# An encoder layer with product-key experts: two token tiles' heads chosen inside the query slabs, and the products' scratch laid out by tile

## The reference, cut to what matters

```python
q = jnp.einsum('td,de->te', x, wq).reshape(T, PEER_HEADS, 2, PEER_DHALF)       # 8 heads, 2 halves of 128
s = jnp.einsum('thcd,hcnd->thcn', q, keys).astype(jnp.float32)                 # 128 keys a half
v1, i1 = lax.top_k(s[:, :, 0], PEER_TOPK)                                      # 16 of each half
v2, i2 = lax.top_k(s[:, :, 1], PEER_TOPK)
cand = (v1[..., :, None] + v2[..., None, :])                                   # 256 sums
top_s, pos = lax.top_k(cand, PEER_TOPK)                                        # 16 of them
idx = i1 * N_KEYS + i2                    # of the 16 chosen; 8 x 16 = 128 experts a token
a = jnp.einsum('td,tkd->tk', xt, u_tab[it])                                    # u_tab: 16384 x 2048
hid = gelu(a) * softmax(top_s)
peer = jnp.einsum('tk,tkd->td', hid, v_tab[it])
x2 = layer_norm(alpha * x1 + peer)
```

## Time and profile before

| | |
|---|---|
| median of three runs | 3742.63 us (3737.31 to 3744.31) |
| the profiled execution | 3735.37 us |
| its span | 3733.6 us, mean granted TensorE clock 0.82 of full speed |
| busy share of the span | PE 66%, PE's weight loads 51%, DVE 74%, ACT 9%, POOL 33% |
| DMA | 1332.43 MB, mean 357 GB/s |

### The profile page before, as it was taken

One profiled execution on the slowest core, in us unless ns is written; L12 is line 12 of the kernel. 1 busy time (PEld: TensorE's weight loads), 2 busy tenths in 40 slices (PEclk: granted clock), 3 DMA queues, 4 the chain that ended last, 5 costly groups with the idle time before them and its releaser, 6 DMA issues.

```text
span 3733.6 us, 30440 instructions
## 1 busy us (share of the span) xinstructions
PE 2471.0 (66%) x11208; PEld 1892.2 (51%) x11208; DVE 2762.9 (74%) x3210; ACT 332.7 (9%) x832; POOL 1246.5 (33%) x1273
## 2 busy tenths in 40 slices
PE   7798799978975777959988999999978000000000
PEld 7687689545743444535677877777767000000000
DVE  5331220979989997787789889976655999988888
ACT  1212311000002221000100000000000000000000
POOL 2420000122233332223222223232222577777772
PEclk9899899988986657989999999999999555555555
DMA  8774355898998999989999999999998999999998
GB/s 245 219 232 121 143 190 179 292 397 332 341 405 343 406 419 375 422 343 414 421 422 423 423 423 423 423 421 424 423 382 336 413 407 410 409 390 370 392 373 348
DMA packets 297908, 1332.43 MB, mean 357 GB/s; under 512 B 70752, under 2 KB 136832, under 8 KB 146336
## 3 DMA queue, kind: packets, MB, share of 16 engines
q0 software_dynamic: 138624, 945.22, 62.9%
q1 hardware_dynamic: 126400, 371.83, 26.7%
q10 hardware_dynamic: 32736, 13.44, 1.4%
HBM read 1282.60 MB, written 57.20 MB: 359 GB/s over the span
## 4 chain that ended last, share of the span: by engine, by line
PE 35%; DMA 27%; DVE 22%; POOL 8%; issue 6%; another core or an unknown queue 1%; ACT 1%; ACTq 1%; SPq 0%; DVEq 0%; POOLq 0%
PE low L1559 18%; DMA arena<-in_ut 16%; PE low L1900 10%; DVE arena L1375 7%; DVE acc L1391 5%; DMA arena<-in_peer_v,arena 5%; POOL arena L611 4%; POOL arena L620 4%; DMA arena<-in_w 2%; DMA arena<-in_peer_u,arena 2%; PE low L1633 1%; PE acc L1633 1%; DMA arena<-y_scratch_b 1%; DVE low L1391 1%
## 5 line engine op out<-in xcount | busy, mean ns | idle before, releaser
L1391 DVE SCALAR_TENSOR_TENSOR acc<-arena,acc 128x2048 f32<-128x2048 f32 x443 | 1042.6, 2354 | 262.4 <-DMA arena<-in_peer_v,arena 226.7
L1559 PE MATMUL low<-arena 128*128 128x192 f32 (+1 forms) x4096 | 1064.8, 420 | 100.6 <-DMA arena<-in_w 77.3
L1900 PE MATMUL low<-arena 128*128 128x256 f32 x4096 | 915.5, 383 | 110.1 <-DMA arena<-in_ut 109.0
L1559 PEld LDWEIGHTS low<-arena 128*128 128x128 f32 x4096 | 738.3, 196 | 376.0 <-DMA arena<-in_w 74.6
L1900 PEld LDWEIGHTS low<-arena 128*128 128x128 f32 x4096 | 774.1, 191 | 251.3 <-DMA arena<-in_ut 133.2
L611 POOL DMA_INDIRECT arena<-in_peer_v,arena x576 | 579.5, 1006 | 924.3 <-DVE acc L1391 772.6
L1375 DVE SCALAR_TENSOR_TENSOR arena<-arena,acc 128x2048 f32<-128x2048 f32 x320 | 724.8, 2284 | 115.3 <-DMA arena<-in_peer_u,arena 107.6
L611 POOL DMA_INDIRECT arena<-in_peer_u,arena x320 | 320.1, 1000 | 1185.6 <-DVE arena L1375 856.1
L1391 DVE SCALAR_TENSOR_TENSOR low<-arena,low 128x2048 f32<-128x2048 f32 x126 | 296.6, 2354 | 35.8 <-DMA arena<-in_peer_v,arena 26.8
L620 POOL DMA_INDIRECT arena<-expert_scratch,arena x256 | 263.3, 1029 | 83.2 <-issue 83.2
L872 ACT COPY arena<-low 128x256 f32<-128x256 f32 x128 | 47.6, 372 | 971.0 <-PE low L1900 957.9
(11 more groups left out here) (274 smaller groups left out, 1678.3 us busy)
## 6 DMA issues: line engine op xcount, KB each, us to landing
arena<-in_w SPq DMA_DIRECT2D x128, 1024.0 KB
arena<-in_ut SPq DMA_DIRECT2D x128, 1024.0 KB
expert_scratch<-arena SPq DMA_DIRECT2D x128, 128.0 KB
arena<-in_peer_v,arena POOLq DMA_INDIRECT x576
arena<-toeplitz_scratch SPq DMA_DIRECT2D x64, 128.0 KB, 3.6
arena<-c_scratch SPq DMA_DIRECT2D x64, 128.0 KB, 4.2
bias_scratch<-distance_scratch SPq DMA_DIRECT2D x1, 5120.0 KB, 23.4
x_scratch<-arena ACTq DMA_DIRECT2D x5, 1024.0 KB
```

Of the source, the lines that this page charges most:

```text
L1391: stt(held, slot[j], wv_, held, ALU.mult, ALU.add).then_inc(used, 1)
L1559: ins = mm(L[n % 2][:, 0:width], wring[n % 2][:, k, :], rhs(k), start=k == 0, stop=k == KT - 1)
L1900: ins = mm(L[j % 4][:, 0:NSD], ud[j % 4][:, k, :], lane(catB, k)[:, P:NB], start=k == 0, stop=k == KT - 1)
```

## The change

1. **Tile 0.** A quarter of the scores is computed as soon as its four query slabs are out: `quarter(t, c)` stands inside slabs 4, 8 and 12 of the 16 (counted from 0), behind their fifth matmul, and after the last. The quarters go to PSUM banks `L[2]` and `L[3]` in turn instead of `acc`. DVE waits for a quarter, chooses its two heads and decodes them, and works no row before all eight are done; then 56 rows follow ahead of the scan, where 14 stood between the heads and 28 behind. Slots 2 and 3 may hold rows from row 2 on instead of row 16.
2. **Tile 2.** The same in group B's query slabs. DVE works 11 rows and, ahead of each pair of heads, 9; the heads are decoded one by one (`decode_head`) instead of in one `decode` with rows between its steps. POOL waits for each head of tile 2 as for those of tile 0 (`chosen`).
3. **The products' scratch** has tile 3's products in its first 8 MB and tile 4's in the second, each [expert in block][block][token]. ACT copies two blocks into one of two buffers, and SP stores the pair at once: 64 DMAs of 256 KB in pieces of 1 KB. The index of a product is computed to match (`idxe`, `tok_off`).
4. **The five loads of `early_sums`** stand at blocks 92, 98, 104, 110 and 116 instead of all at 116.
5. **ACT's root** of the second norm of tile 0 stands behind the 122nd block of the products instead of the 126th.

The diff, cut:

```diff
@@ -97,7 +97,7 @@
 NR = len(ROWS)
-SLOT_FROM = [0, 0, TOPK, TOPK, STEPS[0] + 6, R_U2 + 16]
+SLOT_FROM = [0, 0, 2, 2, STEPS[0] + 6, R_U2 + 16]
@@ -132,6 +132,11 @@
     return u % 3 if u < NUA else u % 2
+def chosen(t, h=PH - 1):
+    return {0: h + 1, 1: PH + 1, 2: PH + 2 + h, 3: 2 * PH + 2, 4: 2 * PH + 3}[t]
@@ -286,7 +291,7 @@
         ud = [at(WO + D * j, D).rearrange("p (k e) -> p k e", k=KT) for j in range(4)]
-        astg = [at(H2 + D + NSD * j, NSD) for j in range(4)]
+        astg = [at(H2 + D + 2 * NSD * j, 2 * NSD).rearrange("p (u n) -> p u n", u=2) for j in range(2)]
@@ -304,7 +309,7 @@
         vscr = nc.dram_tensor("v_scratch", [2, P, D], F32).ap()
-        ascr = nc.dram_tensor("expert_scratch", [EB * P * NSD, 1], F32).ap()
+        ascr = nc.dram_tensor("expert_scratch", [2 * P * EB * P, 1], F32).ap()
@@ -524,31 +530,39 @@
                 sp.dma_start(ud[j % 4].rearrange("p k e -> p (k e)"), a["ut"][j]).then_inc(ud_in[j % 4], 16)
-            def products_out(j):
-                sp.wait_ge(a_out, j + 1)
-                sp.dma_start(ascr.rearrange("(j p t) o -> j p (t o)", p=P, t=NSD)[j], astg[j % 4]
-                             ).then_inc(a_st[j % 4], 16)
+            def products_out(b):
+                sp.wait_ge(a_out, 2 * b + 2)
+                sp.dma_start(ascr.rearrange("(u p b n) o -> b p u (n o)", u=2, p=P, n=2 * P)[b], astg[b % 2]
+                             ).then_inc(a_st[b % 2], 16)
             def early_sums():
-                sp.wait_ge(idx_ready, PH + NT - 1)
+                sp.wait_ge(idx_ready, chosen(NT - 1))
                 sp.wait_ge(v_stored, 32)
                 sp.dma_start(x1f[0], x1scr[0]).then_inc(early_in, 16)
+                yield
                 sp.dma_start(vsum[0], vscr[0]).then_inc(early_in, 16)
+                yield
                 sp.dma_start(x1f[1][0:TS], x1scr[1, 0:TS, :]).then_inc(early_in, 16)
+                yield
                 sp.dma_start(vsum[1][0:TS], vscr[1, 0:TS, :]).then_inc(early_in, 16)
+                yield
                 sp.dma_start(vsum[2][0:TS], vscr[1, TS:P, :]).then_inc(early_in, 16)
+                yield
+            sums = early_sums()
             for j in range(EB):
                 experts_in(j)
-                if j >= 4:
-                    products_out(j - 4)
-                if j == EB - 12:
-                    early_sums()
+                if j >= 5 and j % 2:
+                    products_out((j - 5) // 2)
+                if j in range(EB - 36, EB - 11, 6):
+                    next(sums)
...
-            for j in range(EB - 4, EB):
-                products_out(j)
+            for b in range(EB // 2 - 2, EB // 2):
+                products_out(b)
@@ -593,9 +607,12 @@
                     if s % TOPK == 0:
-                        pool.wait_ge(idx_ready, s // TOPK + 1)
+                        pool.wait_ge(idx_ready, chosen(0, s // TOPK))
+                elif kind == "u" and t == 2:
+                    if s % TOPK == 0:
+                        pool.wait_ge(idx_ready, chosen(2, s // TOPK))
                 elif s == 0 and kind == "u" or i == R_V3 or i == R_V4:
-                    pool.wait_ge(idx_ready, PH + t)
+                    pool.wait_ge(idx_ready, chosen(t))
@@ -837,10 +854,18 @@
                 act.dma_start(x1scr[t], x1s[t]).then_inc(x1_stored, 16)
+            def quarter(t, c):
+                act.wait_ge(score_done, 4 * t + c + 1)
+                if t == NGA and not c:
+                    act.wait_ge(x1_stored, 16 * NT)
+                ins = nc.scalar.copy(scored[t][:, 512 * c:512 * c + 512], L[2 + c % 2])
+                ins.then_inc(quarter_out, 1)
+                if c == 3:
+                    act.wait_ge(quarter_out, 4 * (t // 2) + 4)
+                    act.sem_inc(score_out, 1)
             def scores(t):
                 src = acc if t < NGA else low
-                if t == NGA:
-                    act.wait_ge(x1_stored, 16 * NT)
@@ -867,9 +892,10 @@
                     act.wait_ge(ud_used, j + 1)
-                    if j >= 4:
-                        act.wait_ge(a_st[j % 4], 16 * (j // 4))
-                    nc.scalar.copy(astg[j % 4], L[j % 4][:, 0:NSD]).then_inc(a_out, 1)
+                    if j >= 4 and j % 2 == 0:
+                        act.wait_ge(a_st[j // 2 % 2], 16 * (j // 4))
+                    nc.scalar.copy(astg[j // 2 % 2].rearrange("p u (i t) -> p i u t", i=2)[:, j % 2],
+                                   L[j % 4][:, 0:NSD].rearrange("p (u t) -> p u t", u=2)).then_inc(a_out, 1)
@@ -895,7 +923,7 @@
             mixed_a(N_WA)
-            scores(0)
+            quarter(0, 3)
@@ -997,8 +1025,12 @@
             ln1_out(4)
-            slabs_out(N_WB, 16, mixB, NB)
-            for t in range(NGA, NT):
+            for i in range(16):
+                if i and i % 4 == 0:
+                    quarter(2, i // 4 - 1)
+                out_of(N_WB + i, mixB[:, i, :], L[i % 2][:, 0:NB])
+            quarter(2, 3)
+            for t in range(NGU, NT):
@@ -1009,9 +1041,9 @@
             gates(4)
-            products(106, EB - 2)
+            products(106, EB - 6)
             ln2(0, 0)
-            products(EB - 2, EB)
+            products(EB - 6, EB)
@@ -1294,8 +1326,8 @@
                     flat = pos2[:, 0:KK]
-                    link(stt(flat, row[0], float(NKEY), row[1], ALU.mult, ALU.add))
-                    link(ts_(idxe[:, KK * (t - NGU):KK * (t - NGU) + KK], flat, float(NSD),
+                    link(stt(flat, row[1], float(NKEY), row[0], ALU.mult, ALU.add))
+                    link(ts_(idxe[:, KK * (t - NGU):KK * (t - NGU) + KK], flat, float(P),
@@ -1435,15 +1467,14 @@
             dve.wait_ge(keys_in, 32)
-            dve.wait_ge(score_out, 1)
             for h in range(PH):
+                if h % 2 == 0:
+                    dve.wait_ge(quarter_out, h // 2 + 1)
                 head(0, h)
                 decode_head(0, h)
-                if h:
-                    rows(2)
             logits(0)
             link.zero()
-            rows(28)
+            rows(56)
@@ -1509,13 +1540,16 @@
                 rows(2)
-            rows(53)
+            rows(11)
             dve.wait_ge(keys_in, 48)
-            dve.wait_ge(score_out, 3)
             for h in range(PH):
-                rows(5)
+                if h % 2 == 0:
+                    rows(9)
+                    dve.wait_ge(quarter_out, 4 + h // 2 + 1)
                 head(2, h)
-            decode(2, rows)
+                decode_head(2, h)
+            logits(2)
+            link.zero()
@@ -1758,13 +1792,32 @@
                 c0 = MIXCOL[t] - base
-                if t:
+                if t > 1:
...
+            def quarter(t, c, qp, base, keys):
+                first = (N_WA, N_WB)[t // 2]
+                c0 = MIXCOL[t] - base
+                pe.wait_ge(slab_out, first + 4 * c + 4)
+                pe.wait_ge(keys_in, 32 + 16 * (t // 2))
+                if c >= 2:
+                    pe.wait_ge(quarter_out, 4 * (t // 2) + c - 1)
+                for q in range(4):
+                    ins = mm(L[2 + c % 2][:, P * q:P * q + P], qp[:, 4 * c + q, c0:c0 + P],
+                             keys[:, P * (4 * c + q):P * (4 * c + q) + P], start=True, stop=True)
+                ins.then_inc(score_done, 1)
+            def queries(i, t, qp, base, keys):
+                def between(k):
+                    if k == 4 and i and i % 4 == 0:
+                        quarter(t, i // 4 - 1, qp, base, keys)
+                return between
@@ -1780,12 +1833,10 @@
             pe.wait_ge(x1t_out, 8)
+            pe.wait_ge(res_ready, 2)
             for i in range(16):
-                slab(N_WA + i, ca, NA)
-            pe.wait_ge(slab_out, N_WA + 16)
-            pe.wait_ge(keys_in, 32)
-            pe.wait_ge(res_ready, 2)
-            scores(0, mixA, 0, keysA, acc)
+                slab(N_WA + i, ca, NA, queries(i, 0, mixA, 0, keysA))
+            quarter(0, 3, mixA, 0, keysA)
@@ -1937,7 +1987,7 @@
         "ut": f["peer_u"][0].reshape(EB, P, KT, P).transpose(0, 3, 2, 1).reshape(EB, P, D),
-        "tok_off": np.stack([np.arange(P), np.arange(P) + P], axis=1).astype(np.float32),
+        "tok_off": np.stack([np.arange(P), np.arange(P) + P * EB * P], axis=1).astype(np.float32),
```

More of the change, by code:

```diff
@@ L633, in _ @@
                     sum_store(1)
-            pool.wait_ge(idx_ready, PH + NT - 1)
-            for b in range(4):
+            pool.wait_ge(idx_ready, chosen(NT - 1))
+            for b in range(2):
                 pool.wait_ge(a_st[b], 16 * EB // 4)
@@ L880, in mixed_a @@
                 for i in range(16):
+                    if first == N_WA and i and i % 4 == 0:
+                        quarter(0, i // 4 - 1)
                     act.wait_ge(slab_done, first + i + 1)
@@ L1888, in _ @@
             for i in range(16):
-                slab(N_WB + i, cb, NB)
-            pe.wait_ge(slab_out, N_WB + 16)
-            pe.wait_ge(keys_in, 48)
-            for t in range(NGA, NT):
```

(3 more changed lines are left out.)

3 lines of the change are left out of this document (2 added, 1 removed).

## The result

The changed kernel takes 3805.38 us (median of four runs, 3793.36 to 3812.08); the kernel before took 3740.49 in the same comparison (four runs, 3737.31 to 3744.31). The ratio is 1.0169, 95% interval 1.0141 to 1.0198: **65 us slower**, where 3754 was forecast and 3777 was the range's end.

A forecast was written before the change was run, and what follows sets the result against it. The prediction took full DMA engines from 1687 us on as the bound. Its terms, 18 - 2 - 5 with 0 for the scratch, gave +11 us on 3742.6, so 3754 us, range 3725 to 3777.

The forecast's parts named there:

- What bounds the kernel: From 1687 us on, full DMA engines: remaining time is bytes left, so bytes moved earlier into idle DMA time count.
- Part 1, the scan's start (+18): Tile 0: 14 more rows before the scan delay its start by 18 us, between +7 and +31.
- the forecast 15 us of waiting for DVE: Before the scan's result, PE would idle some 15 us waiting for DVE, against 1.56 us before.
- Part 1, the lead (-35, spent by part 2): After the scan: 14 rows ahead, worth 35 us if kept to the end, but spent during tile 2's heads.
- rival 1: The lead survives because slot prefetch covers tile 2's pairs of heads: -24 us, 3719 us; chance 0.13.
- Part 2 (-2): Tile 2's heads in group B's slabs: lead spent, 8 us missing set against a norm stall; -2 us (-9 to +6).
- Part 3 (-5): Sums: spreading the five loads recovers DMA time lost in the burst, -5 us (0 to -9).
- The root: Tile 0's second norm: root four blocks earlier removes DVE's 24.68 us wait there; DVE waits at tile 1's norm instead.
- Part 4 (0): Products' scratch: same bytes and pieces in 64 issues instead of 128, wide strides not slow; 0 us.
- rival 4: Strided scratch stores run at half rate, 40 us more of a full stage: 3794 us; chance 0.06.
- Rival 3: Tail's gathers of single products for tile 4 reach 410 GB/s through the new layout: -26 us, 3728; chance 0.13.
- The forecast of signs: Whole kernel against 0.2%: faster 0.26, no change 0.28, slower 0.46.

The follow-up runs named there:

- e15: e12 with 18 more rows ahead of the second norms of tiles 0 and 1 on DVE: 3728.14 us, ratio 0.9958.
- e16: e5 with 18 more rows ahead of the second norms of tiles 0 and 1 on DVE: 3728.06 us, ratio 0.9961.
- e14: e12 with the products' scratch of the kernel before: 3763.76 us, ratio 1.0061.
- e9: The changed kernel with slots 2 and 3 back to holding rows from row 16 on: 3762.38 us, ratio 1.0064.
- e12: Kernel before with tile 0's part but old slots, tile 2's quarters in query slabs, DVE's old order there, and scratch by tile: 3740.53 us, ratio 1.0003.
- e4: The changed kernel with POOL issuing no row gather before group B's u has been moved: 3795.95 us, ratio 1.0151.
- e1: Kernel before with part 1 alone, new slots included, and 39 rows instead of 53 ahead of tile 2's heads: 3817.06 us, ratio 1.0200.
- e2: Kernel before with part 2 alone, tile 2's quarters in group B's query slabs and heads in pairs: 3764.84 us, ratio 1.0071.
- e6: Kernel before with only the five loads of the sums spread over blocks 92 to 116: 3737.57 us, ratio 0.9992.
- e7: Kernel before with only ACT's root of tile 0's second norm four blocks earlier: 3738.54 us, ratio 1.0005.
- e5: Kernel before with only the products' scratch by tile, stored in pairs of blocks: 3716.04 us, ratio 0.9950.
- e8: The changed kernel with 5 or 4 rows ahead of every head of tile 2 instead of 9 per pair: 3798.62 us, ratio 1.0179.
- e10: e5 with each pair of blocks stored by two transfers of 128 KB, one per tile: 3729.24 us, ratio 0.9980.
- e3: Kernel before with the three end parts alone (scratch by tile in pairs, spread loads, earlier root): 3724.34 us, ratio 0.9966.
- e13: e12 with the five loads spread and ACT's root earlier too: 3743.89 us, ratio 1.0014.
- e11: Scratch by tile as in e5, with one buffer of four blocks and 32 stores of 512 KB: 3732.24 us, ratio 0.9986.

## Why the prediction was wrong, point by point

**One relation of the profiles carries it.** From the scan's start to PE's first block it is 1033.5 us before, 1037.6 after, and between 1031 and 1042 in each of the sixteen experiments, however many rows DVE has done. From the root of tile 1's norm to the end it is 832 to 839 us in all profiles but e15's and e16's, where the norm was moved. Between them lie PE's blocks, 955 to 1018 us. So what counts is when the scan starts and how long PE's blocks take; DVE's rows count only where they, and not PE, are the later at the norms. How many rows are done earlier counted nothing in these runs.

- **What bounds the kernel.** "From there on the time is the number of bytes left" was wrong. The DMA engines are full from 1687 to 2400, but not through 2850 to 2950 (338 GB/s before), where DVE waited for PE, and that join sets the end. Bytes moved early went into waits for PE's stream: in e14 DVE stands 30 us ahead at row 576, then waits 20.96 us for the sums, which are loaded at PE's block 116, and 55.42 at the norm (24.68 before), where PE's end comes 28 us later.
- **Part 1, the scan's start (+18).** Measured +81 with four slots. With two it is +26 to +28 counted from the first row (e9, e12 to e15), inside "between +7 and +31", so the term as it was worked out was right in size for a kernel without the new slots. The step that failed is "the gathers of rows 0 and 1 can be issued from then on, as before; those of 2 and 3 wait for the eighth head", priced at nothing beyond bytes. Four gathers in flight over the very stretch in which ACT moves u was the new collision. I had excluded PE ("has nothing to do with it at first") without reading what ACT issues at 680 to 735; PE's 41 and 70 us of waiting for ACT stood in place of the forecast 15 us of waiting for DVE. e9 puts 43 us on it, and e4 shows the moves unharmed when nothing else is in flight.
- **Part 1, the lead (-35, spent by part 2).** e1 and e12 show that it was not to be had, and rival 1 with it. That the forecast, 3754, lies near e9's 3762 is luck: the sum used up the lead at row 342, so that the +18 stood alone.
- **Part 2 (-2).** The 330 GB/s of a cycle of heads and rows was right (336, 335 and 279 in e2). That it costs only what the lead held was wrong: a lead had no value at the join of the two chains, and nothing could be paid with it. Alone part 2 costs 27 us: 64 us on DVE less the wait that hid a part of them.
- **Part 3 (-5).** 0 us by the medians of e6, with an interval of -8 to +3: no gain that can be told from none, and -5 lies within. The hole of 27 us vanished, 406 GB/s moved from 2750 to 2850 where 384 did, but PE's blocks took 1014 us against 1011.
- **The root.** Right: it moved the wait to the other norm and nothing else (e7).
- **Part 4 (0).** The sign of rival 4 was wrong and 0 was too. The rule of the Trainium skill ("DMA: Bandwidth & Descriptors", "Latency and other measured facts") is on the pitch from one partition's row to the next. These stores step 64 KB there, less than the smallest pitch that it lists, and only their halves are 8 MB apart; so its loss at 8 MiB does not speak of them, and I had applied it wrongly. e5 moved 422 to 423 GB/s through the blocks and was 22 us faster. I had written that it is 64 issues instead of 128 and priced an issue at nothing.
- **Rival 3 (gathers of products).** In e5 the engines moved 392 GB/s in 3290 to 3430 where 372 stood, and from the root of tile 1 its tail is 833.6 us; but after moved 398 there and its tail is as long as before's (838.5): 0 to 6 us, not 26.
- **The forecast of signs.** Slower was right, but not for the reason given; the range ended 28 us short, since no rival had ACT in it.

## What to carry to other kernels

When a change lets transfers start earlier or more of them be in flight, list every queue that issues in that stretch, the small ones on ScalarE too, and who stands behind the issuing engine: here 32 moves of 48 KB held ACT, ACT held PE, and PE held the scan. Where two chains share DMA engines and meet at one point, work banked in one of them is worth nothing if the other is late; find the meeting point first (here a wait of 24.7 us at a norm), and count from there. And a part put at 0 deserves its own run: the only clear gain of this change lay in one.

## What the runs showed of the hardware

- The time to issue sixteen transfers of 48 KB from ACT's queue: 8.61 us with no gather in flight, 14.50 with rows between the heads, 18.57 to 20.63 with two gathers in flight (e9, e12 to e15), 87.62, 70.06 and 70.42 with four (after, e1, e8). With four, the moves' packets and the gathers' go nearly one for one; with two, six for one (e9). Why, beyond the reading given with e9, stays open.
- The number of store transfers on the queue that also loads a stream went with the stream's pace: PE's 128 blocks took 1009 to 1018 us with 128 stores of 128 KB, in the old layout (before, e1, e2, e6, e7, e14) and the new (e10); 994 to 1005 with 64 of 256 KB (e3 to e5, e8, e9, e12, e13, e15, e16 and after); and 955 with 32 of 512 KB (e11).
- Stores in 1 KB pieces 64 KB apart, in two halves 8 MB apart, ran beside loads and gathers at 422 to 423 GB/s.
